# Sorted work items with a second, 128-slot loop in the mixture-of-experts stage of a one-core trunk kernel

## What is computed

```python
logits = (h @ w_router + b_router)               # 1024 tokens x 32 experts
top_val, top_idx = lax.top_k(logits, TOP_K)      # TOP_K = 4
gate = softmax(top_val)
...
gu = xblk @ w_gate_up[e] + b_gate_up[e]          # 1024 -> 2 x 1024
g_lin = minimum(gu[:, :1024], 7); u_lin = clip(gu[:, 1024:], -7, 7)
act = g_lin * sigmoid(1.702 * g_lin) * (u_lin + 1)
y += gate * (act @ w_down[e] + b_down[e])        # 1024 -> 1024, added to the token's row
```

## Time and profile before

| | before |
|---|---|
| median of 3 runs | 2249.86 us (2248.14 to 2250.61) |
| the profiled execution | 2252.61 us, its span 2250.7 us |
| PE busy | 2116.3 us, 94% of the span |
| PE weight loads busy | 1796.4 us, 80% |
| DVE busy | 1548.6 us, 69% |
| ACT busy | 1412.7 us, 63% |
| the matmuls of the expert stage (L1580) | 18432, busy 1300.1 us |
| granted TensorE clock | 0.964 of full on average |

### The profile page before, as it was taken

One profiled execution on the slowest core, in us unless ns is written; L12 is line 12 of the kernel. 1 busy time (PEld: TensorE's weight loads), 2 busy tenths in 40 slices (PEclk: granted clock), 3 DMA queues, 4 the chain that ended last, 5 costly groups with the idle time before them and its releaser, 6 DMA issues.

```text
span 2250.7 us, 59693 instructions
## 1 busy us (share of the span) xinstructions
PE 2116.3 (94%) x24537; PEld 1796.4 (80%) x24537; DVE 1548.6 (69%) x1933; ACT 1412.7 (63%) x1633; POOL 604.2 (27%) x379
## 2 busy tenths in 40 slices
PE   5999999999937958999999999999999999999998
PEld 3444864344813548999999999999999999999997
DVE  5331424444673247888888888888888888888886
ACT  4331315564263346787777778778777877877884
POOL 2221212222050122322332332242233224223221
PEclk7999999999958969999999999999999999999999
DMA  4111100000031267898898998989889898988987
GB/s 159 38 46 48 57 1 1 0 1 1 30 121 50 84 238 260 311 326 315 316 327 306 329 316 315 328 314 328 307 317 326 311 334 313 329 308 317 325 307 239
DMA packets 142564, 489.40 MB, mean 217 GB/s; under 512 B 12794, under 2 KB 27898, under 8 KB 142448
## 3 DMA queue, kind: packets, MB, share of 16 engines
q1 hardware_dynamic: 129648, 444.78, 54.0%
q0 software_dynamic: 12864, 43.88, 8.2%
HBM read 457.34 MB, written 35.52 MB: 219 GB/s over the span
## 4 chain that ended last, share of the span: by engine, by line
PE 57%; DVE 3%; DMA 2%; issue 1%; ACT 1%; POOL 0%; POOLq 0%; DVEq 0%; SPq 0%; ACTq 0%
PE banks L1580 52%; PE banks L1574 3%; DVE region_c L1412 2%; PE banks L1560 1%; DMA rows_out<-region_b 1%; PE banks L1547 1%; DMA region_d<-w_down_dram 0%; DMA region_b<-rows_out,region_d 0%; ACT region_b L1267 0%; DMA rows_out<-region_b,region_d 0%; DVE region_b L1438 0%; ACT region_b L1253 0%; ACT region_b L1263 0%; POOL rows_out L1185 0%; POOL region_b L1177 0%
## 5 line engine op out<-in xcount | busy, mean ns | idle before, releaser
L1580 PE MATMUL banks<-region_b,region_c 128*128 128x160 f16 x18432 | 1300.1, 233 | 8.6 <-DVE region_c L1412 5.9
L1580 PEld LDWEIGHTS banks<-region_b,region_c 128*128 128x128 f16 x18432 | 1281.3, 98 | 12.9 <-DVE region_c L1412 7.0
L1412 DVE TENSOR_TENSOR region_c<-region_a,region_c 128x4096 f16<-128x4096 f32 x128 | 565.5, 4418 | 28.5 <-ACT region_c L1247 14.4
L1247 ACT ACTIVATE region_c<-region_a 128x4096 f16<-128x4096 f32 x128 | 462.5, 3613 | 52.1 <-DMA region_a<-w_gate_up_dram 52.1
L1181 POOL DMA_INDIRECT region_b<-rows_h,region_d x64 | 294.3, 4598 | 35.8 <-issue 28.8
L1247 ACT ACTIVATE region_c<-region_d 128x4096 f16<-128x4096 f32 x64 | 231.5, 3618 | 100.6 <-DMA region_d<-w_gate_up_dram 63.8
L1412 DVE TENSOR_TENSOR region_c<-region_d,region_c 128x4096 f16<-128x4096 f32 x64 | 282.5, 4414 | 2.7 <-ACT region_c L1247 2.7
L1190 POOL TENSOR_TENSOR region_d<-region_d 80x1 f32<-80x1 f32 x96 | 20.2, 210 | 923.6 <-DVE region_d L1389 656.8
L345 PE MATMUL banks<-region_a,region_d 128*128 128x512 f16 x960 | 210.9, 382 | 7.8 <-POOL region_d L319 7.8
L345 PEld LDWEIGHTS banks<-region_a,region_d 128*128 128x128 f16 x960 | 94.6, 99 | 124.3 <-POOL region_d L319 8.2
L1276 ACT ACTIVATE region_b<-banks,region_d 80x512 f32<-80x512 f32 x128 | 80.4, 678 | 138.8 <-PE banks L1574 125.7
(11 more groups left out here) (246 smaller groups left out, 2214.9 us busy)
## 6 DMA issues: line engine op xcount, KB each, us to landing
region_a<-w_gate_up_dram SPq DMA_DIRECT2D x192, 1024.0 KB
region_d<-w_gate_up_dram SPq DMA_DIRECT2D x64, 1024.0 KB
region_a<-w_down_dram SPq DMA_DIRECT2D x64, 1024.0 KB
region_d<-w_down_dram SPq DMA_DIRECT2D x64, 1024.0 KB
region_d<-w_in_dram SPq DMA_DIRECT2D x14, 1024.0 KB, 5.0
region_b<-x_dram SPq DMA_DIRECT2D x8, 1024.0 KB, 8.7
region_c<-w_out_dram SPq DMA_DIRECT2D x8, 512.0 KB, 3.6
rows_out<-region_b SPq DMA_DIRECT2D x8, 512.0 KB, 2.7
```

Source lines behind the costliest of these rows:

```text
L1247: act.activation(part_hi[r], raw[r], ACT.Copy).then_inc(s_hi9, 1)
L1412: dve.tensor_tensor(part_lo[r], raw[r], part_hi[r], ALU.subtract).then_inc(s_lod, 1)
L1580: mm = pe.matmul(out_ap, a, b, start=(first and s == 0), stop=(k == KT - 1 and s == 2), skip_group_check=True)
```

## The change

The items are sorted: first those whose expert has more than 128 tokens (and any rest past 160), then the others. Expert 0 is always put with the first (its threshold is overwritten with -1). A third number goes into `table`, the count of the first kind (`count_wide`). PE, DVE and ACT run the first kind in a loop with `width` = `SL` = 160, and then the others in a second loop, and the last item, with `width` = `NARROW` = 128: matmuls stream 128 columns, and what DVE and ACT read and make of gate, up, activation and down has 128 slots. SyncE and GpSimd keep one loop. Chunks, ring, gathers, scatters, `turn_x`, `turn_y`, `find`, `choose`, `x_split` and `y_rows` keep their sizes. The `Fori` lines stand alike on the three engines.

```diff
-        ITEMS = NE + T * TOPK // SL
+        ITEMS = NE + T * TOPK // SL + 2
+        NARROW = P
...
+        def slots(t, f0, f1, width):
+            return t[:, f0 * SL:f1 * SL].rearrange("p (f t) -> p f t", t=SL)[:, :, 0:width]
...
+        def count_wide(eng):
+            return eng.value_load(table[0:1, 2 * TAB + 2:2 * TAB + 3], min_val=1, max_val=ITEMS - 2)
...
+                pool.memset(thr[:, 0:1], float(NARROW)).then_inc(s_p8, 1)
+                pool.wait_ge(s_p8, 11)
+                pool.affine_select(out=thr[:, 0:1], in_=thr[:, 0:1], compare_op=ALU.is_gt, fill=-1.0, base=0, pattern=[[0, 1]],
+                                   channel_multiplier=1).then_inc(s_p8, 1)
...
-                    act.activation(sig_all[:, f0 * SL:f1 * SL], g_all[:, f0 * SL:f1 * SL], ACT.Sigmoid, scale=1.702).then_inc(s_sig, 1)
+                    act.activation(slots(sig_all, f0, f1, width), slots(g_all, f0, f1, width), ACT.Sigmoid, scale=1.702).then_inc(s_sig, 1)
...
-                with act.Fori(0, n_last) as i:
-                    item(i, False)
-                item(n_last, True)
+                n_wide = count_wide(act)
+                with act.Fori(0, n_wide) as i:
+                    item(i, False, SL)
+                with act.Fori(n_wide, n_last) as i:
+                    item(i, False, NARROW)
+                item(n_last, True, NARROW)
...
-                    dve.tensor_scalar(g_all[:, f * SL:f * SL + SL], tile_at(0, f), b_cur[:, f:f + 1], 7.0, ALU.add, ALU.min).then_inc(s_gev, 1)
+                    dve.tensor_scalar(g_all[:, f * SL:f * SL + width], tile_at(0, f)[:, 0:width], b_cur[:, f:f + 1], 7.0, ALU.add, ALU.min).then_inc(s_gev, 1)
...
+                dve.tensor_tensor(over[0:NE, 0:MORE + 1], thr[0:NE, :], bank[3][0:NE, 0:1].to_broadcast([NE, MORE + 1]), ALU.is_lt)
+                dve.tensor_tensor(over[0:NE, MORE + 1:KINDS], thr[0:NE, 0:1], bank[3][0:NE, 0:1], ALU.is_ge).then_inc(s_over, 1)
...
-                choose(1, 0)
                 dve.wait_ge(s_table, 1)
+                choose(dve.value_load(table[0:1, 1:2], min_val=0, max_val=NE - 1),
+                       dve.value_load(table[0:1, TAB + 1:TAB + 2], min_val=0, max_val=(MAXC - 1) * SL))
...
-                def product(out_ap, r, f, kk, k, hi, lo, first):
+                def product(tile, width, r, f, kk, k, hi, lo, first):
+                    out_ap, hi, lo = tile[:, 0:width], hi[:, :, 0:width], lo[:, :, 0:width]
```

More of the change, by code:

```diff
@@ L1292, in _, with item @@
                 n_items, n_last = count_items(act)
-                def item(i, last):
+                def item(i, last, width):
                     act.wait_ge(s_dn, i * 16 + C1)
@@ new lines, in _ @@
+                dve.tensor_copy(table[:, 2 * TAB + 2:2 * TAB + 3], totals[0:1, 0:1])
+                dve.tensor_scalar(past[0:1, :], iota[0:1, 0:TAB], totals[0:1, 1:2], float((MAXC - 1) * SL), ALU.is_ge, ALU.mult)
+                link(dve.scalar_tensor_tensor(out=n_all[0:1, :], in0=totals[0:1, 0:1], scalar=2.0, in1=totals[0:1, 1:2],
+                                              op0=ALU.add, op1=ALU.max))
+                dve.tensor_copy(table[:, 2 * TAB:2 * TAB + 1], n_all[0:1, :])
+                dve.tensor_scalar(table[:, 2 * TAB + 1:2 * TAB + 2], n_all[0:1, :], -1.0, None, ALU.add)
@@ L1504, in item @@
                         low_part(i * CH + 7, 7)
-                with dve.Fori(0, n_last) as i:
-                    item(i, False)
-                item(n_last, True)
+                n_wide = count_wide(dve)
+                with dve.Fori(0, n_wide) as i:
+                    item(i, False, SL)
+                with dve.Fori(n_wide, n_last) as i:
+                    item(i, False, NARROW)
+                item(n_last, True, NARROW)
                 dve.wait_ge(s_yrow, n_items * 4 + C1)
@@ L1581, in product, with gate @@
                     return mm
-                def gate(i, half):
+                def gate(i, half, width):
                     pe.wait_ge(s_lod, i * CH + (half + 1))
@@ L1591, in gate, with up @@
                                 pe.wait_ge(s_xlo, i * 2 + (half + 1))
-                            mm = product(tile_at(0, f), half, f, kk, half * HK + kk, xT_hi, xT_lo, half == 0 and kk == 0 and f % TPB == 0)
+                            mm = product(tile_at(0, f), width, half, f, kk, half * HK + kk, xT_hi, xT_lo, half == 0 and kk == 0 and f % TPB == 0)
                         mm.then_inc(s_g, 1)
-                def up(i, half, last):
+                def up(i, half, last, width):
                     pe.wait_ge(s_lod, i * CH + (2 + half + 1))
@@ L1615, in down @@
                                     pe.wait_ge(s_alo, i * 4 + (k // 2 + 1))
-                                mm = product(tile_at(0, f), (4 + half) % RING, f, kk, k, aT_hi, aT_lo, k == 0 and f % TPB == 0)
+                                mm = product(tile_at(0, f), width, (4 + half) % RING, f, kk, k, aT_hi, aT_lo, k == 0 and f % TPB == 0)
                             if k1 == 4:
@@ L1641, in _, with item @@
                 n_items, n_last = count_items(pe)
-                def item(i, last):
-                    gate(i, 0)
+                def item(i, last, width):
+                    gate(i, 0, width)
                     if not last:
@@ L1648, in item @@
                     turn_y(i, 1)
-                    gate(i, 1)
+                    gate(i, 1, width)
                     turn_y(i, 2)
                     turn_y(i, 3)
-                    up(i, 0, last)
-                    up(i, 1, last)
+                    up(i, 0, last, width)
+                    up(i, 1, last, width)
                     pe.wait_ge(s_yrow, i * 4 + (4 + C1))
@@ L1656, in item @@
                         turn_x(i + 1, 0)
-                    down(i, 0)
+                    down(i, 0, width)
                     if not last:
                         turn_x(i + 1, 1)
-                    down(i, 1)
-                with pe.Fori(0, n_last) as i:
-                    item(i, False)
-                item(n_last, True)
+                    down(i, 1, width)
+                n_wide = count_wide(pe)
+                with pe.Fori(0, n_wide) as i:
+                    item(i, False, SL)
+                with pe.Fori(n_wide, n_last) as i:
+                    item(i, False, NARROW)
+                item(n_last, True, NARROW)
                 for g in range(4):
```

122 lines of the change are left out of this document (59 added, 63 removed).

## The result

The changed kernel takes 2222.9 us (median of 4 runs, 2219.1 to 2233.4) against 2249.1 before (4 runs, 2248.1 to 2250.6): ratio 0.9892, 95% interval [0.9862, 0.9922]. That is 26 us or 1.1% less, clear of the interval. The forecast was 2207, 42 to 43 us less, in a range of 2162 to 2236.

A forecast was written before the change was run, and what follows sets the result against it. PE bounds the kernel at 43.5 us an item; narrow items fall to 41.1, set by chunk loads. Gains 1.3 + 38.7 + 3.7 less 0.3 are 43.4 us: 2252.6 to 2209.2, median 2207, range 2162 to 2236.

The forecast's parts named there:

- The bound: Items before the change: PE sets the pace at 43.5 us, with DMA at 39.7 and DVE at 37.7 close behind.
- A narrow matmul, 55.8 ns: PE in narrow items: a 128-column matmul takes 55.8 ns instead of 69.2, so PE's own work is 35.8 us.
- the rival in which the weight load keeps a matmul at 69.2 ns: PE's narrow matmuls: the weight load, not the columns, sets their time, so the change does nothing; 2250 us, 4%.
- the rival in which narrow matmuls are slower than wide ones: PE's narrow matmuls: 128-column pairs take longer than 69.2 ns, at 81 ns 2366 us; slower had 6%.
- DVE saves 1.2 us, ACT 0.7, beside the path: DVE and ACT in a narrow item: 128 slots save 1.2 and some 0.7 us; DVE's busy time falls to 36.5.
- The loads take over as the bound: Narrow items: the chunk-load ring, hidden behind PE before, sets the pace at 41.1 us; 50% for within 1 us.
- the ring through PE and DVE: Narrow item, find to L5, then down half 1 and gate half 0: 38.5 us, deciding if loads keep up; 2165 us, 15%.
- The ring's sum, 41.1 us: Narrow item, from L2's end through loads, H7, y_copy, gate half 0 and find to L2's end: 23.96+5.63+5.36+0.61+1.13+4.41 = 41.1 us.
- A wait takes the place: Narrow items: an earlier turn_x meets the second gather, or crowded chunks need 1 us more; 42.1 us, 2222 us, 8%.
- Where PE waits: PE in a narrow item: 5.3 us of waits, about 2.3 before down half 1 and as much before gate half 0.
- The clock: PE's clock falls to 0.50 after waits, losing 1.6 us ahead of gate half 0: 42.7 us an item, about 2232, 13%.
- The last item, 3.7 us: Last item, L2 to L5 and down half 1: DVE saves 1.2 and some 1.2 of waits, down half 1 1.3; 3.7 us.

The follow-up runs named there:

- pe_wide: Changed kernel with PE kept at 160 columns in the second loop, only DVE and ACT narrow: 2247.6 us, ratio 0.9990 to before.
- pe_only: Changed kernel with only PE narrow in the second loop, DVE and ACT kept at 160 slots: 2217.3 us, ratio 0.9857 to before.
- half_loads: Changed kernel with half the weight bytes moved by each load behind the first three chunks: 2162.0 us, ratio 0.9608 to before.
- again: The changed kernel run once more, unaltered: 2221.3 us, ratio 0.9875 to before.
- warm: Changed kernel with 48 unused 128-column PE matmuls added ahead of down half 0 in narrow items: 2223.3 us, ratio 0.9876 to before.
- pe_short: Changed kernel with only PE narrow in the second loop, and gathers and scatters there only up to slot 127: 2226.6 us, ratio 0.9888 to before.
- few_scatter: Changed kernel with each scatter moving 16 of its 80 rows, in all items: 2212.5 us, ratio 0.9849 to before.
- few_gather: Changed kernel with each gather fetching 16 of its 80 rows, in all items: 2203.1 us, ratio 0.9793 to before.
- short_rows: Changed kernel with the second gather and scatter of narrow items moving 48 rows instead of 80: 2214.9 us, ratio 0.9856 to before.
- h5_late: Changed kernel with ACT's high part of chunk 5 moved behind up_read and the first two act_high, all items: 2331.5 us, ratio 1.0371 to before.

## Why the forecast was right, and where its size was off

**The bound.** Right. Wide items stayed at 43.5, and pe_wide shows that narrower DVE and ACT work alone does not shorten an item (43.4 us); PE's does.

**A narrow matmul, 55.8 ns.** Right: 56.2 ns. So the rival in which the weight load keeps a matmul at 69.2 ns falls. The Trainium skill, page "TensorE: Matmul & The Clock Gate", section "Back-to-back issue gap", gives about 81 ns for a weight load and matmul pair with 128 columns. This case's trace doesn't agree, with the 56.2 ns above, and the rival in which narrow matmuls are slower than wide ones falls too.

**DVE saves 1.2 us, ACT 0.7, beside the path.** Right in that pe_only loses nothing; pe_wide gains 0.1%, no more than its interval. Share times period in the rows of 1500 to 2100 gives DVE 37.5 us an item before and 36.3 after, ACT 34.0 and 32.9: 1.2 and 1.1 less.

**The loads take over as the bound.** Right: half_loads moves narrow items from 42.0 to 39.0 us, close to where the ring through PE and DVE was put, 38.5. DMA work an item, share times period, is 0.93 x 42.5 = 39.5 us in the changed kernel against 39.7 before: the amount is the same, the idle part of it shrank from 3.8 us to 3.0, and to about 2 in pe_only. The loads are not alone in it: without four fifths of the gathers narrow items took 41.1 us.

**The ring's sum, 41.1 us.** This term was mis-sized: 42.5 us in the first profile, 42.0 in the second, 41.5 in pe_only. Its parts, over 15 narrow items of the first profile, in the prediction's order: from the end of L2 to H7 24.7 us on average (forecast 23.96), from H7 over `y_copy` and gate half 0 to `find` 11.2 (5.63 + 5.36 = 11.0), from `find` to the end of L2 6.7 (0.61 + 1.13 + 4.41 = 6.15). In pe_only they are 24.0, 11.25 and 6.15, the forecast to 0.3 us. So the ring was found, and what it missed is that the stretch of loads and the start of the item do not keep their length when the timing around them moves. In the changed kernel the stretch goes from 21.9 to 27.0 us, in pe_only from 23.6 to 25.5. The start got longer where DVE waited for a scatter to land (2.45 us in the row above). Against 41.1, 42.0 to 42.5 us are 0.9 to 1.4 us an item, so 14 to 22 us over 16 items, beside the 16 us by which the median missed the forecast. In spans of the profiled executions the change is worth 19.1 us: the 16 steps give 16.6 (the forecast had 40, with the first half of 1.3), the end of the kernel -0.8 (forecast 3.7), and 3.4 us come from before item 14's `find`, which the forecast had at -0.3. That last part is no gain that can be claimed: the same `find` stands at 1461.7 us before, 1458.4 here and 1462.7 in pe_only.

**The rival that came nearest.** "A wait takes the place" (8%) had as one of its two reasons that the chunks need 1 us more as gather, scatter and loads crowd, 42.1 us an item and 2222. The measured 42.0 to 42.5 us and 2222.9 are its numbers, and the longer stretch of loads (24.2 and 24.7 us) is 0.2 to 0.7 of that 1 us; the later start of the item is the rest. The forecast named the ring, this rival its size.

**Where PE waits.** Half wrong: I divided 5.3 us into 2.3 before gate half 0 and 2.3 before down half 1, and left out the wait before down half 0, because I took H5's chunk to be there when ACT came to it. Its load was late, and ACT's list made `up_read` late with it. In the longer items this is one wait of up to 6 us. In the even items of pe_only, and in three of 40.9 to 41.3 us in again, all three places show: 1.9 to 2.6 us before down half 0, 1.2 to 1.5 before down half 1 where the clock stayed up, 0.8 to 1.4 before gate half 0 for `y_copy`, where the sum of the ring ends. The changed kernel's first profile has that last wait in one narrow item only, with 0.6 us.

**The clock.** It was a rival (13%, 2232 us), and the clock did fall in 13 of the 16 items behind waits of 2.8 to 6.0 us, and stayed up behind three of 1.9 to 2.1. The prediction had named a clock below 1.00 in narrow items as a sign of being wrong; the sign came, and bound and ring still held, so it was no good sign. warm and the even items of pe_only show that the clock is not what costs: where a load decides, PE may run slowly. In pe_only it fell behind waits of 2.0 to 2.6 us in eight items and stayed up behind waits of 1.9 to 2.6 in five, so the length of the wait alone does not tell. The price I had put on it, 1.6 us an item on the ring, was wrong in its place, since the low clock fell on down half 0 and not on gate half 0.

**The last item, 3.7 us.** Wrong. From the last `find` (2138.37) to the end of the span are 93.2 us, before (2158.30) 92.4. `shift` after L5 lets GpSimd read the last rows of `rows_out`, and DVE waited for them, so the narrower down half 1 has no say in the end:

```profile
2207.31 4.42 DVE L1426 TENSOR_TENSOR region_c<-region_d,region_c 128x4096 f16<-128x4096 f32 x1
2211.64 0.16 DVE L1533 COPY region_d<-region_d 80x2 f32<-80x2 f32 x1
...
2223.38 1.40 DVE L1541 SCALAR_TENSOR_TENSOR region_b<-banks,region_d,region_b 80x512 f32<-80x512 f32 x2 [11.51 <-DMA region_b<-rows_out,region_d]
```

L5 ended 29.3 us after gate half 0 did, before 29.2, since H5 waited for its load here too. Down half 1 lay beside that 11.5 us wait all along, so its 1.3 us could not count. The same stretch, from the last `find` to the end, varies more than the term is large: 93.8 us in again, 89.6 in pe_only, 95.8 in pe_short.

Open: why pe_only, few_scatter, few_gather and short_rows had shorter narrow items than the same kind of kernel on the other chips, 41.1 to 41.5 against 42.0 to 42.5; why the stretch of loads is uneven in the changed kernel and even in pe_only; and why some scatter issues are held and others, at the same distance from `low_part`, are not. No version here is faster than the changed kernel by more than the measurement can tell, with nothing left out.

## What to carry to other kernels

When the busiest engine has others at nine tenths behind it, the worth of making it faster is set by these, and is read by following each ring of waits to the same point in the next item; here PE's work fell by 7.7 us an item and the item, with nothing left out, by 1.0 to 2.3. A ring's stretch of DMA is no constant: take its mean, and widen it upwards where the DMA share is above nine tenths, as here. Narrow the bounding engine first and alone: DVE's and ACT's share of this change was worth nothing that could be measured.

## What the hardware showed that was not expected

An indirect DMA on GpSimd can take longer to issue when one of DVE's `low_part` instructions (128x4096, 4.4 us) runs beside it. All 58 gathers of the kernel before between 900 and 2140 us began under a `low_part` and ended 0.8 us behind its end; most took 4.6 to 4.9 us. With L2 in two instructions of 2.3 us they took 2.5 and 1.9 in wide items. Six gathers of the changed kernel began with no `low_part` running, and took 0.9. Scatter issues took 5.6 to 7.1 us or 1.4 to 1.8. The ten long ones of the changed kernel began 0.03 to 0.04 us before a `low_part` or 0.14 us behind its start, but four others that began 0.03 to 0.04 us before one took 1.4, so this does not yet tell which will be held. A `nop` with an increment placed behind such an issue on GpSimd's list let DVE go 0.03 us after the issue began. And a granted clock of 0.50 for 75 us of 630 cost nothing that can be measured, because the engine it slows was not the one waited for; in a wide item of h5_late, where it was, the same level cost 2.9 us.
